# The scores of a compressed attention branch: keys in four column groups, queries moving, then two transposes

## The chip, the cores and the metric

The kernel runs on one core of one Trainium2 chip. The metric is the device time of one execution in microseconds (us); lower is better. Engines are named as in the profile: PE is TensorE, PEld its weight loads, DVE is VectorE, ACT is ScalarE, POOL is GpSimd, SP is SyncE, whose queue issues the weight DMAs.

## The reference, cut to what matters

The program is one block of a first architecture followed by two layers of a second one, on 256 tokens (S) of width 1024. Each layer of the second kind has a feed-forward part, a mixer with three attention branches, and a second feed-forward part. The change is in the mixer's second branch, in the part that attends to compressed keys:

```python
kc = rms_norm_2(nsa_compress(k_cmp, pe[0], w1[0], w2[0]), k_norm[0])   # (B, 15, 2 groups, 64)
kc = apply_rope(kc, cos_c, sin_c).transpose(0, 2, 1, 3)
...
sc = jnp.einsum('btghd,bgcd->bghtc', qb, kc) * scale     # 8 heads, 256 queries, 15 keys
pc = masked_softmax(sc, cmp_end[None, :] <= t_pos[:, None])
o_cmp = jnp.einsum('bghtc,bgcd->btghd', pc.astype(dt), vc)
```

So the scores are 8 heads by 256 queries by 15 compressed keys, with two key groups of four heads each, and the softmax runs over the 15 keys. They are computed once in each of the two layers, and all operands are float32.

## The kernel before, in words

**Weights.** All weights come in units of 1 MB that SP loads into three `raw` slots. ACT copies each into `w_hi` in a shortened format (`split_hi`, L253, 1.9 us), DVE subtracts that from the raw data into `w_lo` (`split_lo`, L260, 2.3 us), and PE multiplies with three products per tile (L818, L819, L820 in the projections). There are four slots of `w_hi` and `w_lo`. `ahead(i)` in the mixer is the split of unit u0+i+2; it stands at fixed places in the programs of ACT and DVE.

**Order.** Each engine has its own program, written out by hand, and runs it strictly in that order; the engines meet through semaphores. In `pe_mix2` the projections are cut into quarters of 12 matmuls (`quarter`, `tile`), and smaller work stands between them. `pe_items` transposes query and key pairs into PSUM banks 4 to 7, one bank for each item; ACT and DVE copy the items out in turn (`evac_items`, L886 on ACT, L888 on DVE, one with the even item numbers, the other with the odd ones). `pe_items_left` makes PE wait until all items are copied out. The next users of those banks are the attention scores.

**Around the change.** After quarter (6, 1, 0) PE waits for the copies of the first three query/key items, transposes two more (`qk_items[3:]`, six transposes at L868), computes the compressed scores (L1899), waits in `pe_items_left` and goes into `pe_attention`. There the step i issues the scores of block i (L908), `beside(i, 0)` (a quarter, then small work of the compressed branch), the transposes of the probabilities of block i-1 (L958), `beside(i, 1)` (another quarter), and the product with the values of block i-2 (L986).

The compressed scores before: for each of two token tiles and four head pairs one matmul with a 128x128 tile of queries (`qk_t[:, i, t*P:(t+1)*P]`) standing and `kc_t` moving. `kc_t` is 128 rows by 30 columns: rows 0 to 63 hold one group's 15 keys, rows 64 to 127 the other's, the rest is zero. The result lies in bank 3 as tokens by (head, key), as the softmax on DVE wants it (`cmp_shift`, L2269 to L2273, in DVE's step 0 after the maxima of block 0 (L919) and ahead of a weight split, L260).

On ACT the program runs here: copies of `qk_items[:3]` (L886), `ahead(12)` (L253), the copy of `qk_items[3:]` (L886), then in step 0 of the attention `ahead(13)` (L253) and the exponentials of block 0 (L928). On DVE: `evac_items` (L888), L1735, `ahead(12)` (L260), two gate operations, the maxima of block 0 (L919), `cmp_shift`, `ahead(13)` (L260), then step 1: reciprocals and scaled probabilities of block 0 (L998 to L1004). POOL zeroes `kc_t` at the start of the mixer (L1772), and ACT writes the transposed keys into it (L2035). The two layers differ in one thing that matters here: which of ACT and DVE has the even items, so the last item that ACT copies is 128x256 in the first layer and 128x512 in the second.

Other lines that the rows name: L1813 is the matmul in `hidden(k)`, four products with 32 standing columns each, placed in four column groups of the array by `tile_position`; L1922 is the pair of transposes of the compressed probabilities; L566 and L567 are the gate and up products of the first feed-forward part; L1188 and L1203 belong to the first block's attention; L423 is a residual addition.

Of the kernel before, what the change touches and what calls it, by code (L numbers as in the profile page):

```python
# [21 lines left out]
ALU = mybir.AluOpType  # L22
ACT = mybir.ActivationFunctionType
AX = mybir.AxisListType

P = 128
S = 256
NT = S // P
# [77 lines left out]
def build(nc, A, place, out):  # L106

    with ExitStack() as ctx:
# [18 lines left out]
        x = sb("x", [P, NT, D])  # L127
        tmp = sb("tmp", [P, 2176])
        qk_t = sb("qk_t", [P, 16, S])
# [9 lines left out]
        small = sb("small", [P, 656])  # L139
        forget_hi, forget_lo = (sb(f"forget_{i}", [P, KC * 8], F32R) for i in ("hi", "lo"))  # L140
        ps = ctx.enter_context(nc.psum_tensor("ps", [P, 8, 512], F32))
# [7 lines left out]
        def const(name, rows=P):  # L149
            a, w = place[name]  # L150
            return consts[0:rows, a:a + w]

        ident = const("ident")
# [46 lines left out]
        for ph in phases:  # L200
            ph = dict(ph)
# [675 lines left out]
        def evac_items(eng, st, items, parity, bank=0):  # L877
            for i, (srcs, dst, scale) in enumerate(items):
                m = st["item"] + i
                if m % 2 != parity:  # L880
                    continue
                eng.wait_ge(items_done, m + 1)
                n = len(srcs)
                src = ps[:, bank + i % 4, 0:n * S].rearrange("p (h s) -> p h s", h=n)
                if parity == 0:
                    nc.scalar.activation(dst, src, ACT.Copy, scale=scale).then_inc(item_act, 1)  # L886
                else:
                    nc.vector.tensor_scalar(dst, src, scale, None, ALU.mult).then_inc(item_dve, 1)  # L888
            st["item"] += len(items)
# [631 lines left out]
        SBH, NH, NG, DSH, IXH, IXD = 4, 8, 2, 4, 8, 32  # L1521
        NQ, NKC, NKS, NVS, NKW, NVW, GATES, DQ, DV0, IQ, IW = (768, 1280, 1536, 1664, 1792, 1920, 2048, 2072,
                                                               2392, 2456, 2744)
        NB = S // 16 - 1
# [14 lines left out]
        ptb = pt_buf[:, :, :, :].rearrange("p a b c -> p (a b c)")  # L1539
# [7 lines left out]
        kc_pair = small[0:2 * NB, 260:388]  # L1547
        kc_sq = small[0:2 * NB, 324:388]
        kc_ss = small[0:2 * NB, 388:389]
        kc_t = small[:, 390:390 + 2 * NB]  # L1550
        kc_rot = small[0:2 * NB, 420:452]
        nsa_gate = tiny(452, [NT, 3 * NH])
        gates = nsa_gate.rearrange("p t (h c) -> p t h c", c=3)
# [8 lines left out]
        cmp_s = qk_t[:, 11, 0:NT * NH * NB].rearrange("p (t h c) -> p t h c", t=NT, h=NH)  # L1562
# [4 lines left out]
        SIDE_BANK, CMP_BANK = 2, 3  # L1567

        def ev(name, ph):

            return sem(name), ph["mix2_before"] + 1

        def wait(eng, name, ph, times=1):
            s_, v_ = ev(name, ph)
            eng.wait_ge(s_, v_ * times)
# [193 lines left out]
            nc.gpsimd.memset(cmp_in[:, :, :, 2 * NB:32], 0.0).then_inc(ev("cmp_in_zeroed", ph)[0], 1)  # L1769

        def pool_mix2(pool, chain, ph):
            nc.gpsimd.memset(kc_t, 0.0).then_inc(ev("kct_zeroed", ph)[0], 1)  # L1772
            for i, (_, _, h0, n) in enumerate((qk_first, qk_second, qk_dsa)):
                ss = qk_ss[:, :, h0:h0 + n]
                pool.wait_ge(sem("qk_ss_ready"), 3 * ph["mix2_before"] + i + 1)
                nc.gpsimd.tensor_tensor(ss, ss, minus_half.unsqueeze(2).broadcast_to([P, NT, n]), ALU.pow)\
                    .then_inc(sem("qk_rstd_ready"), 1)
                if i == 0:
                    wait(pool, "kc_ss_ready", ph)
                    nc.gpsimd.tensor_tensor(kc_ss, kc_ss, minus_half[0:2 * NB], ALU.pow)\  # L1780
                        .then_inc(ev("kc_rstd_ready", ph)[0], 1)
            for t in range(NT):
                for h in range(2):
                    pool.wait_ge(sem("gated1"), 4 * ph["mix2_before"] + 2 * t + h + 1)
                    nc.gpsimd.tensor_tensor(xn[:, t, half(h)], gate_or_gain[:, t, half(h)],
                                            gate_or_gain[:, t, D + h * 512:D + (h + 1) * 512], ALU.add)\
                        .then_inc(sem("merged_ab"), 1)

        def pe_mix2(pe, ph):
# [44 lines left out]
            for a in range(2):  # L1834
                for g in range(NG):
                    for t in range(NT):
                        for par in range(2):
                            c = (a * NG + g) * P + t * HD
                            last = nc.tensor.matmul(ps[par * HD:(par + 1) * HD, SIDE_BANK, c:c + HD],
                                                    proj[:, t, NKC + (a * NG + g) * HD:NKC + (a * NG + g + 1) * HD],  # L1840
                                                    ident[:, par::2], start=True, stop=True)
# [20 lines left out]
                             start=True, stop=True)  # L1862
# [12 lines left out]
            for c in range(2):  # L1875
                for kt in range(NT):
                    for hh in range(2):
                        h = 2 * c + hh
                        last = nc.tensor.matmul(half_rows(o_sb[:, c, :], hh)[:, kt * P:S],
                                                proj[:, kt, 512 + h * HD:512 + (h + 1) * HD],  # L1880
                                                sb_view(pb, c)[:, hh, kt * S:kt * S + S - kt * P],
                                                start=kt == 0, stop=True, skip_group_check=True)
# [10 lines left out]
            wait(pe, "dk_ready", ph)  # L1893
            pe_items(pe, st, qk_items[3:], 4)
            wait(pe, "kcT_ready", ph, 2)
            for t in range(NT):
                for i in range(NH // 2):
                    c = (t * NH + 2 * i) * NB
                    last = nc.tensor.matmul(ps[:, CMP_BANK, c:c + 2 * NB], qk_t[:, i, t * P:(t + 1) * P],  # L1899
                                            kc_t, start=True, stop=True)  # L1900
            last.then_inc(ev("cmp_scores", ph)[0], 1)
            pe_items_left(pe, st)

            def branch(n, bank, first, last, t, rows_of=None):
# [5 lines left out]
            def beside(i, place):  # L1910
                j = 2 * i + place + 3
                if j < 24:
                    quarter(6 + j // 4, j % 4 // 2, j % 2)
                elif place == 0 and i > 10:
                    pe.wait_ge(proj_evac, pj0 + 24)
                    branch(23, 0, True, True, 0, "branch_rows0")
                if place:
                    return
                if i == 3:
                    wait(pe, "cmp_p_ready", ph)  # L1920
                    for t in range(NT):
                        last = nc.tensor.transpose(ps[0:NH * NB, CMP_BANK, t * P:(t + 1) * P],  # L1922
                                                   cmp_s[:, t].rearrange("p h c -> p (h c)"), ident)
                    last.then_inc(ev("cmp_pt", ph)[0], 1)
                if i in (4, 6, 8, 10):
                    c = i // 2 - 2
                    wait(pe, "cmp_pt_ready", ph)
                    nc.tensor.matmul(o_psum(c), v_diag.rearrange("p h d -> p (h d)")[:, c * P:(c + 1) * P], cmp_p_t,
                                     start=False, stop=True, skip_group_check=True).then_inc(sem("nsa_closed"), 1)
# [18 lines left out]
        def act_mix2(act, chain, ph):  # L1948
            st, u0, li = {"item": ph["item0"]}, ph["u0"], ph["mix2_before"]

            def ahead(i):
                split_hi(act, u0 + i + 2)
# [80 lines left out]
            for hh in range(2):  # L2033
                c = slice(hh * NB, (hh + 1) * NB)
# [5 lines left out]
            nc.scalar.activation(nsa_gate, nsa_gate, ACT.Exp, scale=-1.0).then_inc(ev("gates_exp", ph)[0], 1)  # L2040
            evac(6, 0)
            evac_items(act, st, qk_items[:3], 0, 4)
            ahead(12)
            evac_items(act, st, qk_items[3:], 0, 4)

# [36 lines left out]
        def dve_mix2(dve, chain, ph):  # L2082
# [81 lines left out]
            for a in range(2):  # L2164
                for g in range(NG):
                    c = (a * NG + g) * P
                    pairs = ps[:, SIDE_BANK, c:c + P].rearrange("p (m j) -> p m j", j=8)
                    for jh in range(2):
                        last = nc.vector.tensor_tensor(
                            cmp_in[:, a, 8 * jh:8 * jh + 8, g * NB:(g + 1) * NB].rearrange("p j c -> p c j"),  # L2170
                            pairs[:, jh:jh + NB, :],
                            cmp_pe[:, a, 8 * jh:8 * jh + 8].unsqueeze(1).broadcast_to([P, NB, 8]), ALU.add)
# [88 lines left out]

            shape = [P, NT, NH, NB]
            vis = const("cmpvis").rearrange("p (t c) -> p t c", t=NT).unsqueeze(2).broadcast_to(shape)
            bias = const("cmpbias").rearrange("p (t c) -> p t c", t=NT).unsqueeze(2).broadcast_to(shape)

            def cmp_shift():
                wait(dve, "cmp_scores", ph)
                sc = ps[:, CMP_BANK, 0:NT * NH * NB].rearrange("p (t h c) -> p t h c", t=NT, h=NH)
                chain(nc.vector.tensor_tensor(cmp_s, sc, bias, ALU.add))  # L2269
                chain.wait()  # L2270
                chain(nc.vector.tensor_reduce(cmp_max, cmp_s, AX.X, ALU.max))
                chain.wait()
                nc.vector.tensor_tensor(cmp_s, cmp_s, cmp_max.unsqueeze(3).broadcast_to(shape), ALU.subtract)\  # L2273
                    .then_inc(ev("cmp_shifted", ph)[0], 1)
# [17 lines left out]

            def beside(i, place):
                if place == 0:
                    if i == 0:
                        cmp_shift()
                    if i <= 10:
                        ahead(13 + i)
                    return
                if i == 1:  # L2300
                    cmp_softmax()
                if 1 <= i <= 5:
                    top_k(2 + i, 3 + i)
                if i == 6:
                    mask_from_taken()
# [204 lines left out]
```

## Time and profile before

| | |
|---|---|
| median of 3 runs | 1708.38 us (1708.22 to 1708.61) |
| the profiled execution | 1708.45 us, its span 1706.3 us |
| PE busy | 1694.1 us, 99% of the span |
| DVE busy | 1022.8 us, 60% |
| ACT busy | 840.0 us, 49% |
| POOL busy | 109.1 us, 6% |
| DMA | mean 176 GB/s |

The span is the time from the first to the last instruction that the profiler records; the run's own time has 2.15 us more around it. Busy shares are averages over the whole program; a matmul's duration in the trace runs to its modelled end, so matmuls that follow each other every 0.23 us have 0.39 us each.

### The profile page before, as it was taken

How to read it: one execution, taken by the hardware profiler on the slowest of the kernel's cores; microseconds unless marked ns; L12 is line 12 of the kernel's file. 1: busy time of each engine (PE TensorE's matmuls, PEld its weight loads, DVE VectorE, ACT ScalarE, POOL GpSimd, SP SyncE). 2: the span in 40 equal slices, each digit the busy share in tenths (PEclk: the TensorE clock that was granted, in tenths of full speed). 3: DMA queues.
4: the chain of work that ended last, by engine and by line, in shares of the span. 5: the costliest groups of instructions: out<-in, count | busy, mean ns of one | idle time of the engine just before them, and what ended most of it. 6: DMA issues, size and time to landing. Idle time of an engine off the chain costs nothing.

```text
span 1706.3 us, 22051 instructions
## 1 busy us (share of the span) xinstructions
PE 1694.1 (99%) x8308; PEld 1374.5 (81%) x8308; DVE 1022.8 (60%) x1481; ACT 840.0 (49%) x1102; POOL 109.1 (6%) x141
## 2 busy tenths in 40 slices
PE   8999999999999999999999999999999999999999
PEld 6888887788888888878778888888888787788887
DVE  6444756754556454769866545554547698665454
ACT  5444565643454343566664434443435666644342
POOL 2000200200003000100011000020001010110000
PEclk9999999999999999999999999999999999999999
DMA  8555542455557555534344554565555344345542
GB/s 296 184 202 176 173 173 99 166 193 196 180 190 232 195 185 184 197 107 159 131 136 170 189 197 175 195 229 198 176 192 195 104 156 138 129 171 194 197 172 99
DMA packets 69805, 299.87 MB, mean 176 GB/s; under 512 B 5408, under 2 KB 7680, under 8 KB 44512
## 3 DMA queue, kind: packets, MB, share of 16 engines
q1 hardware_dynamic: 66752, 291.52, 49.1%
q0 software_dynamic: 2688, 7.19, 1.4%
q8 instruction: 52, 0.85, 0.2%
q14 instruction: 25, 0.20, 0.0%
q10 hardware_dynamic: 288, 0.10, 0.0%
HBM read 297.74 MB, written 1.05 MB: 175 GB/s over the span
## 4 chain that ended last, share of the span: by engine, by line
PE 98%; DVE 1%; ACT 0%; DMA 0%; issue 0%; POOL 0%; ACTq 0%
PE ps L547 13%; PE ps L545 13%; PE ps L546 13%; PE ps L609 9%; PE ps L611 9%; PE ps L610 9%; PE ps L818 6%; PE ps L820 6%; PE ps L819 6%; PE ps L566 2%; PE ps L567 2%; PE ps L593 2%; PE ps L908 1%; PE ps L986 1%; PE ps L353 1%; PE ps L569 1%
## 5 line engine op out<-in xcount | busy, mean ns | idle before, releaser
L260 DVE TENSOR_TENSOR w_lo<-raw,w_hi 128x2048 fp32r<-128x2048 f32 x275 | 625.0, 2291 | 217.0 <-ACT w_hi L253 216.8
L253 ACT ACTIVATE w_hi<-raw 128x2048 fp32r<-128x2048 f32 x275 | 520.5, 1913 | 59.7 <-PE ps L820 32.5
L545 PE MATMUL ps<-w_hi,aT_hi 128*128 128x512 f32 x960 | 379.4, 395 | 0.0
L547 PE MATMUL ps<-w_hi,aT_lo 128*128 128x512 f32 x960 | 374.6, 390 | 0.0
L546 PE MATMUL ps<-w_lo,aT_hi 128*128 128x512 f32 x960 | 373.9, 389 | 0.0
L703 ACT ACTIVATE tmp<-ps,stats 128x256 f32<-128x256 f32 x132 | 62.6, 474 | 578.9 <-PE ps L547 568.6
L746 DVE TENSOR_TENSOR tmp<-tmp,ps 128x256 f32<-128x256 f32 x132 | 55.6, 421 | 337.4 <-ACT tmp L703 337.2
L609 PE MATMUL ps<-w_hi,act_hi 128*128 128x512 f32 x576 | 226.7, 394 | 0.1
L611 PE MATMUL ps<-w_hi,act_lo 128*128 128x512 f32 x576 | 224.4, 390 | 0.0
L610 PE MATMUL ps<-w_lo,act_hi 128*128 128x512 f32 x576 | 224.3, 389 | 0.0
L547 PEld LDWEIGHTS ps<-w_hi,aT_lo 128*128 128x128 f32 x960 | 180.2, 188 | 38.4
L546 PEld LDWEIGHTS ps<-w_lo,aT_hi 128*128 128x128 f32 x960 | 180.5, 188 | 36.0
L545 PEld LDWEIGHTS ps<-w_hi,aT_hi 128*128 128x128 f32 x960 | 180.4, 188 | 35.6
L818 PE MATMUL ps<-w_hi,aT_hi 128*128 128x512 f32 (+1 forms) x432 | 174.3, 404 | 0.0
L820 PE MATMUL ps<-w_hi,aT_lo 128*128 128x512 f32 (+1 forms) x432 | 165.4, 383 | 0.0
L819 PE MATMUL ps<-w_lo,aT_hi 128*128 128x512 f32 (+1 forms) x432 | 165.4, 383 | 0.0
L609 PEld LDWEIGHTS ps<-w_hi,act_hi 128*128 128x128 f32 x576 | 108.1, 188 | 23.2 <-issue 1.0
L611 PEld LDWEIGHTS ps<-w_hi,act_lo 128*128 128x128 f32 x576 | 108.1, 188 | 22.8
L610 PEld LDWEIGHTS ps<-w_lo,act_hi 128*128 128x128 f32 x576 | 108.2, 188 | 21.8
L818 PEld LDWEIGHTS ps<-w_hi,aT_hi 128*128 128x128 f32 x432 | 81.2, 188 | 27.0 <-issue 11.4
L820 PEld LDWEIGHTS ps<-w_hi,aT_lo 128*128 128x128 f32 x432 | 81.2, 188 | 16.8
L819 PEld LDWEIGHTS ps<-w_lo,aT_hi 128*128 128x128 f32 x432 | 81.4, 189 | 12.9
(296 smaller groups left out, 1605.5 us busy)
## 6 DMA issues: line engine op xcount, KB each, us to landing
raw<-in_ffn_units SPq DMA_DIRECT2D x197, 1024.0 KB, 5.0
raw<-in_w_in SPq DMA_DIRECT2D x34, 1024.0 KB, 5.2
raw<-in_w_gate SPq DMA_DIRECT2D x24, 1024.0 KB, 5.2
raw<-in_w_out SPq DMA_DIRECT2D x12, 1024.0 KB, 4.9
qk_t<-in_nsa_cmp_w POOLq DMA_DIRECT2D x8, 512.0 KB, 5.8
raw<-in_w_br_b SPq DMA_DIRECT2D x4, 1024.0 KB, 5.1
raw<-in_w_br_a SPq DMA_DIRECT2D x2, 1024.0 KB, 4.8
raw<-in_w_br_c SPq DMA_DIRECT2D x2, 1024.0 KB, 5.6
```

What stands on the lines that cost most here:

```text
L253: nc.scalar.activation(w_hi[w][:, :], raw[k][:, :], ACT.Copy).then_inc(hi_ready, 1)
L260: nc.vector.tensor_tensor(w_lo[w][:, :], raw[k][:, :], w_hi[w][:, :].bitcast(F32), ALU.subtract)\
L545: nc.tensor.matmul(dst, aT_hi[:, a, toks], hi[:, k, :], start=a == 0, stop=False)
L546: nc.tensor.matmul(dst, aT_hi[:, a, toks], lo[:, k, :], start=False, stop=False)
L547: last = nc.tensor.matmul(dst, aT_lo[:, a, toks], hi[:, k, :], start=False, stop=a == KC - 1)
L609: nc.tensor.matmul(dst, hi_a[:, c, toks], hi[:, c, cols], start=first and c == 0, stop=False)
L610: nc.tensor.matmul(dst, hi_a[:, c, toks], lo[:, c, cols], start=False, stop=False)
L611: mm = nc.tensor.matmul(dst, lo_a[:, c, toks], hi[:, c, cols], start=False, stop=last and c == 1)
L703: nc.scalar.activation(sg[par][:, t, :], gu(par, t)[:, 0, :], ACT.Silu, scale=rstd(ph, t))\
L818: nc.tensor.matmul(dst, aT_hi[:, a, toks], hi[:, k, :], start=a == 0, stop=False)
L819: nc.tensor.matmul(dst, aT_hi[:, a, toks], lo[:, k, :], start=False, stop=False)
L820: last = nc.tensor.matmul(dst, aT_lo[:, a, toks], hi[:, k, :], start=False, stop=a == KC - 1)
```

## The change

The compressed scores are computed the other way round. `kc_t` (now 32 columns wide, two of them zero) stands, in column group i of the array (`tile_position=(0, 32 * i)`), and all 256 queries of head pair i move; four such matmuls give bank 3 as (pair, key) by tokens. ACT copies this out (`cmp_flat`), and PE transposes it in two 128x128 transposes, after the first quarter in step 0 of the attention. `cmp_shift` on DVE reads these, in one addition for each token tile instead of one for both. `kc_t` moves to columns 80 to 111 of `small`, where `cmp_sig` was, and POOL zeroes it later, once the hidden values are done.

```diff
--- before.py
+++ after.py
@@ -1547,7 +1547,8 @@
         kc_pair = small[0:2 * NB, 260:388]
         kc_sq = small[0:2 * NB, 324:388]
         kc_ss = small[0:2 * NB, 388:389]
-        kc_t = small[:, 390:390 + 2 * NB]
+        kc_t = small[:, 80:112]
+        cmp_flat = ptb[:, 0:S]
         kc_rot = small[0:2 * NB, 420:452]
         nsa_gate = tiny(452, [NT, 3 * NH])
         gates = nsa_gate.rearrange("p t (h c) -> p t h c", c=3)
@@ -1769,13 +1770,14 @@
             nc.gpsimd.memset(cmp_in[:, :, :, 2 * NB:32], 0.0).then_inc(ev("cmp_in_zeroed", ph)[0], 1)
 
         def pool_mix2(pool, chain, ph):
-            nc.gpsimd.memset(kc_t, 0.0).then_inc(ev("kct_zeroed", ph)[0], 1)
             for i, (_, _, h0, n) in enumerate((qk_first, qk_second, qk_dsa)):
                 ss = qk_ss[:, :, h0:h0 + n]
                 pool.wait_ge(sem("qk_ss_ready"), 3 * ph["mix2_before"] + i + 1)
                 nc.gpsimd.tensor_tensor(ss, ss, minus_half.unsqueeze(2).broadcast_to([P, NT, n]), ALU.pow)\
                     .then_inc(sem("qk_rstd_ready"), 1)
                 if i == 0:
+                    wait(pool, "hid_ready", ph)
+                    nc.gpsimd.memset(kc_t, 0.0).then_inc(ev("kct_zeroed", ph)[0], 1)
                     wait(pool, "kc_ss_ready", ph)
                     nc.gpsimd.tensor_tensor(kc_ss, kc_ss, minus_half[0:2 * NB], ALU.pow)\
                         .then_inc(ev("kc_rstd_ready", ph)[0], 1)
@@ -1893,12 +1895,10 @@
             wait(pe, "dk_ready", ph)
             pe_items(pe, st, qk_items[3:], 4)
             wait(pe, "kcT_ready", ph, 2)
-            for t in range(NT):
-                for i in range(NH // 2):
-                    c = (t * NH + 2 * i) * NB
-                    last = nc.tensor.matmul(ps[:, CMP_BANK, c:c + 2 * NB], qk_t[:, i, t * P:(t + 1) * P],
-                                            kc_t, start=True, stop=True)
-            last.then_inc(ev("cmp_scores", ph)[0], 1)
+            for i in range(NH // 2):
+                last = nc.tensor.matmul(ps[32 * i:32 * i + 32, CMP_BANK, 0:S], kc_t, qk_t[:, i, :], start=True, stop=True,
+                                        tile_position=(0, 32 * i))
+            last.then_inc(ev("cmp_flat_done", ph)[0], 1)
             pe_items_left(pe, st)
 
             def branch(n, bank, first, last, t, rows_of=None):
@@ -1916,6 +1916,12 @@
                     branch(23, 0, True, True, 0, "branch_rows0")
                 if place:
                     return
+                if i == 0:
+                    wait(pe, "cmp_flat_ready", ph)
+                    for t in range(NT):
+                        last = nc.tensor.transpose(ps[:, CMP_BANK, S + t * P:S + (t + 1) * P],
+                                                   cmp_flat[:, t * P:(t + 1) * P], ident)
+                    last.then_inc(ev("cmp_scores", ph)[0], 1)
                 if i == 3:
                     wait(pe, "cmp_p_ready", ph)
                     for t in range(NT):
@@ -2040,6 +2046,8 @@
             nc.scalar.activation(nsa_gate, nsa_gate, ACT.Exp, scale=-1.0).then_inc(ev("gates_exp", ph)[0], 1)
             evac(6, 0)
             evac_items(act, st, qk_items[:3], 0, 4)
+            wait(act, "cmp_flat_done", ph)
+            nc.scalar.activation(cmp_flat, ps[:, CMP_BANK, 0:S], ACT.Copy).then_inc(ev("cmp_flat_ready", ph)[0], 1)
             ahead(12)
             evac_items(act, st, qk_items[3:], 0, 4)
 
@@ -2261,12 +2269,16 @@
 
             shape = [P, NT, NH, NB]
             vis = const("cmpvis").rearrange("p (t c) -> p t c", t=NT).unsqueeze(2).broadcast_to(shape)
-            bias = const("cmpbias").rearrange("p (t c) -> p t c", t=NT).unsqueeze(2).broadcast_to(shape)
+            bias = const("cmpbias").rearrange("p (t c) -> p t c", t=NT)
 
             def cmp_shift():
                 wait(dve, "cmp_scores", ph)
-                sc = ps[:, CMP_BANK, 0:NT * NH * NB].rearrange("p (t h c) -> p t h c", t=NT, h=NH)
-                chain(nc.vector.tensor_tensor(cmp_s, sc, bias, ALU.add))
+                sc = ps[:, CMP_BANK, S:2 * S].rearrange("p (t i x) -> p t i x", t=NT, i=NH // 2)
+                for t in range(NT):
+                    chain(nc.vector.tensor_tensor(cmp_s[:, t].rearrange("p (i g) c -> p i g c", g=2),
+                                                  sc[:, t, :, 0:2 * NB].rearrange("p i (g c) -> p i g c", g=2),
+                                                  bias[:, t].unsqueeze(1).unsqueeze(1).broadcast_to([P, NH // 2, 2, NB]),
+                                                  ALU.add))
                 chain.wait()
                 chain(nc.vector.tensor_reduce(cmp_max, cmp_s, AX.X, ALU.max))
                 chain.wait()
@@ -2292,11 +2304,11 @@
 
             def beside(i, place):
                 if place == 0:
-                    if i == 0:
-                        cmp_shift()
                     if i <= 10:
                         ahead(13 + i)
                     return
+                if i == 0:
+                    cmp_shift()
                 if i == 1:
                     cmp_softmax()
                 if 1 <= i <= 5:
```

## Rows read from the trace of the kernel before

**Rows 1.** The page: busy time of PE, its share of the span, instructions.

```profile
PE 1694.1 (99%) x8308; PEld 1374.5 (81%) x8308; DVE 1022.8 (60%) x1481; ACT 840.0 (49%) x1102; POOL 109.1 (6%) x141
```

**Rows 2.** Waits of PE: line waited for, us in total, times, longest us.

```profile
PE ps L353 <- DVE x L423: 1.3, 1, 1.3
```

**Rows 3.** Timeline of PE around the compressed scores: start us, us, what.

```profile
784.58 0.38 PE L868 MATMUL ps<-consts,qk_t 128*128 128x128 f32 x2
784.80 1.87 PE L1899 MATMUL ps<-small,qk_t 128*128 128x30 f32 x16
786.60 0.93 PE L908 MATMUL ps<-qk_t 64*128 64x128 f32 x8
...
790.29 0.39 PE L818 MATMUL ps<-w_hi,aT_hi 128*128 128x512 f32 x1
```

**Rows 4.** A wait of PE's sequencer: nanoseconds min/median/max, first and last start.

```profile
L935 PEldq EVENT_SEMAPHORE  x2: 867/892/918, 784.6 to 1382.6; - x2
```

**Rows 5.** Timeline of PE, a call of "hidden" between projection matmuls.

```profile
738.03 0.39 PE L819 MATMUL ps<-w_lo,aT_hi 128*128 128x512 f32 x1
738.26 0.40 PE L820 MATMUL ps<-w_hi,aT_lo 128*128 128x512 f32 x1
738.59 0.43 PE L1813 MATMUL ps<-qk_t,gate_or_gain 128*32 128x128 f32 x8
738.94 0.50 PE L818 MATMUL ps<-w_hi,aT_hi 128*128 128x512 f32 x1
```

**Rows 6.** PE groups by form: count, busy us, mean ns of one.

```profile
L986 PE MATMUL ps<-pt_buf,proj 128*64 128x128 f32 x96 | 9.3, 273 | 0.0
...
L1928 PE MATMUL ps<-qk_t 120*128 120x256 f32 x16 | 4.8, 378 | 0.0
```

**Rows 7.** Timeline of PE, two transposes ahead of six.

```profile
812.06 0.38 PE L1922 MATMUL ps<-consts,qk_t 128*120 128x128 f32 x2
812.28 0.82 PE L958 MATMUL ps<-consts,p_buf 128*128 128x128 f32 x6
```

**Rows 8.** Timeline of ACT in the first of the two layers.

```profile
785.00 0.38 ACT L886 ACTIVATE qk_t<-ps 128x256 f32<-128x256 f32 x1 [1.03 <-PE ps L868]
785.28 1.90 ACT L253 ACTIVATE w_hi<-raw 128x2048 fp32r<-128x2048 f32 x1
```

**Rows 9.** The producer and PE's first load after an ACT wait.

```profile
297.20 0.37 ACT L1203 ACTIVATE gate_or_gain<-ps 128x256 f32<-128x256 f32 x1
...
297.69 0.30 PEld L1188 LDWEIGHTS ps<-proj,pt_buf 128*128 128x128 f32 x2 [0.22 <-issue]
```

**Rows 10.** Timeline of DVE, first layer.

```profile
785.99 2.28 DVE L260 TENSOR_TENSOR w_lo<-raw,w_hi 128x2048 fp32r<-128x2048 f32 x1
...
790.01 0.40 DVE L2269 TENSOR_TENSOR qk_t<-ps,consts 128x240 f32<-128x240 f32 x1
...
791.21 2.29 DVE L260 TENSOR_TENSOR w_lo<-raw,w_hi 128x2048 fp32r<-128x2048 f32 x1
```

**Rows 11.** DVE, the second block of scaled probabilities.

```profile
802.49 1.01 DVE L1004 TENSOR_SCALAR p_buf<-p_buf,small 128x128 f32<-128x128 f32 x4
```

**Rows 12.** PE, the transposes that read them.

```profile
804.05 0.82 PE L958 MATMUL ps<-consts,p_buf 128*128 128x128 f32 x6
```

**Rows 13.** Timeline of PE and ACT in the second layer.

```profile
1382.60 0.38 PE L868 MATMUL ps<-consts,qk_t 128*128 128x128 f32 x2
...
1382.80 0.60 ACT L886 ACTIVATE qk_t<-ps 128x512 f32<-128x512 f32 x1 [1.24 <-PE ps L868]
...
1384.61 0.93 PE L908 MATMUL ps<-qk_t 64*128 64x128 f32 x8
```

**Rows 14.** The page's DMA issues: KB each, median us to landing.

```profile
raw<-in_w_gate SPq DMA_DIRECT2D x24, 1024.0 KB, 5.2
```

**Rows 15.** Timeline of PE at the start of the program.

```profile
10.94 0.63 PE L566 MATMUL ps<-w_hi,aT_hi 128*128 128x512 f32 x1
11.36 0.50 PE L567 MATMUL ps<-w_lo,aT_hi 128*128 128x512 f32 x1
```

## The prediction, made before the changed kernel ran

> **What bounds the kernel now.** I read the page's busy times first. PE is busy for 1694.1 us of a span of 1706.3 us [rows 1], so the time is PE's time, and a change is worth what it adds to or takes from PE's row of work. Next I read who makes PE wait: after the start of the program the longest wait is 1.3 us [rows 2], so nearly nothing can be won by waiting less, and a new wait shows in full. Then the timeline of PE around the edit. The compressed scores are 16 records, two for each of 8 float32 matmuls. From the second of the two L868 transposes (784.69, one pitch of 0.11 after 784.58) to the first score of the attention (786.60) there are 1.91 us [rows 3]. Last I looked at what else ends there: PE's sequencer sits at the waits of `pe_items_left` and L935 for 0.92 us from 784.60, so until 785.52 [rows 4]. That wait costs nothing today, because the 16 queued records keep the array busy until 786.60. It is the row that decides this case.
>
> **What the new matmuls cost PE.** No row has four 32-column groups with 256 moving columns; the nearest has them with 128. There 8 records start and end within 0.36 us, 738.59 to 738.94 [rows 5], so the four groups run beside each other. Entering the mode costs 0.10 (738.26 to 738.59 is 0.33 against a pitch of 0.23 for 738.03 to 738.26). From 128 to 256 columns a record grows by 0.10 to 0.11 (273 ns to 378 ns [rows 6]), in two rounds, so the block takes 0.36 + 0.21 = 0.57, and its last result lies ready 0.43 + 0.21 = 0.64 after its start. Lower bound of the block: 0.36, as if the columns were free. Upper bound: eight records one after another at 0.21 each, 1.70. I take 0.57, as the row is the same form but for its length.
> The Trainium skill ("TensorEngine Tiling (Array Packing)", Key Properties) says that changing the tiling mode drains the engine; rows 5 show it, 0.10 on the way in, and that is in the sum.
> Start of the block: 784.69 + 0.11 + 0.10 = 784.90. PE would be through at 785.47, 1.13 us earlier than before. That is what the edit takes away.
>
> **What it adds on PE.** Two transposes in step 0 of the attention. A pair takes 0.22 (812.06 to 812.28 [rows 7]) in the same mode as its neighbours, so 0.22 per layer. Were this all, each layer would gain 0.91 us.
>
> **The wait that comes up.** PE must not begin the scores before `pe_items_left`, so not before ACT has copied its last item out of PSUM. ACT runs its program in order, and the edit puts two things ahead of that copy: a wait for the new matmuls, and the copy of their result. But `ahead(12)`, the 1.90 us split, already stood between the first copies and the last one. Before, ACT did that split while PE worked on a quarter, and then idled for 1.03 us until the last item came [rows 8]. Now ACT stands before the split, waiting for PE. Queued behind the waiting copy are the split, the last item's copy, and PE behind that. First layer:
> - matmul result 784.90 + 0.64 = 785.54; ACT starts 0.04 later, as it did after L868 (784.58 + 0.38 to 785.00 [rows 3, 8]), at 785.58;
> - the copy of 128x256 from PSUM: the next instruction starts 0.28 after such a one (785.00 to 785.28 [rows 8]), 785.86;
> - the split: 1.90 [rows 8], less the 0.10 by which neighbours overlap (0.38 against 0.28), 787.66;
> - the last item's copy, 128x256: 0.38 [rows 8], 788.04;
> - to PE's first load after a copy by ACT that it waited for: 297.20 + 0.37 to 297.69, 0.12 [rows 9], 788.15.
> The scores started at 786.60 before [rows 3], so PE is now 1.55 us later, after standing still for 788.15 - 785.47 = 2.7 us.
> Second layer, same steps from 1382.60 + 0.11 + 0.20 = 1382.91: result and ACT's start +0.68, copy +0.28, split +1.80, gives 1385.67. ACT's last item is 128x512 here and takes 0.60 [rows 13]: 1386.27, PE at 1386.38 or so. Before it was 1384.61 [rows 13]: 1.77 us later.
> Bounds of this term: with the block at 0.36 both layers are 0.21 less; with it serial, 1.13 more. The copy cannot overtake the split, so I know of no lower end but that of the rival below.
> The Trainium skill's tiling page (Performance Considerations, PSUM Bottleneck) warns that after a fourfold gain on TensorE the copy out of PSUM may become the bound. By that rule alone the copy's 0.28 to 0.38 would be the price and the layer would still gain; the trace says that the copy is the small part and the 1.80 queued behind it the large one.
>
> **What is hidden.** The last-item delay also moves DVE. Its `ahead(12)` (L260) starts at 785.99 [rows 10] and needs ACT's split, now done at 785.86 + 1.90 = 787.76; it starts at 787.80, 1.81 later. The score maxima follow and end 1.81 later, so `cmp_shift` could start at 790.01 + 1.81 = 791.82 [rows 10]. The two transposes end later: the second quarter of step 0, ahead of which they stand, began at 790.29 [rows 3], now 791.84, they add 0.22 and their latency, 792.2. So DVE waits another 0.4, and its addition, split in two of half the size, costs 0.1 more. `ahead(13)`, at 791.21 before [rows 10], comes some 2.3 later, and all behind it too, DVE having no gap there. PE is later itself by 1.55 + 0.22 = 1.77, so DVE loses 0.5 us against PE. The tightest meeting is in step 2: the scaled probabilities of block 1 run from 802.49 to 803.50 [rows 11], their first half done at about 803.0, and PE takes them at 804.05 [rows 12]. A margin of 1.0 shrinks to 0.5, which holds; without that cover it would cost up to 0.5 a layer per further 1.0 of DVE delay. The weight units have more room: the unit split by `ahead(12)` is used from the second quarter after the second scores on, some 9 us after its split. SP's next load starts when DVE frees the raw slot, 1.8 later, and lands in 5.2 [rows 14], about 795.3, some 5 us ahead of ACT's need in step 2. POOL's zeroing of `kc_t` moves behind the first of its powers; POOL is busy for 6% of the span [rows 1], the write into `kc_t` comes two projection tiles later, and nobody waits for the zeroing. Nothing is priced there.
>
> **The sum.** First layer 1.55 + 0.22, second 1.77 + 0.22: 3.76 us more. The profiled execution has 1706.3 + 2.15 = 1708.45, which is within 0.1 of the median of the runs, 1708.38. Forecast: 1708.38 + 3.76 = 1712.1.
>
> **The rivals.**
> *A. The wait is hidden; not slower.* PE gains 1.13 - 0.22 = 0.91 a layer and the time is 1706.6. It needs ACT's last copy to be done by the time PE leaves the new block: the chain of copy, split and copy would have to be 2.7 us shorter, so the decisive point is whether 788.15 falls below 785.47. For it: before, the same wait was hidden (rows 4). Against it: hidden by the very records that go, and ACT's order is written out. 9 in 100.
> *B. The column groups don't run together at 256 columns.* Then the block takes 1.70, 1.13 more; ACT starts later by that, and with it PE: 3.76 + 2.26, 1714.4. For it: four groups read four different query tiles of 256 columns at once, which no row shows. Against it: rows 5. 5 in 100.
> *C. TensorE's clock falls in the wait.* At the start of the program matmuls of 512 columns follow each other at 0.42 (10.94 to 11.36 [rows 15]), the 1.2 GHz level, against 0.23 later (rows 5), the 2.4 GHz level. If each wait brought the low level back for 4 us, a length I assume, half of that would be lost twice: 1716. For it: waits of 2.7 and 2.9 us are twice the longest that rows 2 hold, and by the Trainium skill ("TensorE: Matmul & The Clock Gate", HAM oscillation) idle gaps that are long enough bring the low clock back. Against it: over the 1.3 us the granted clock stayed at 1.0, and the array is full on both sides. 3 in 100.
> *D. DVE makes PE wait once more.* If its delay is 1 us over what I have, the margin of 0.5 is gone and each layer loses another 0.5: 1713.1. 5 in 100.
>
> **How the numbers follow.** The forecast's own case has 78 in 100; its range is 3.3 to 4.3 above before, 1711.7 to 1712.7, from 0.2 less on the block or the hand-over to some 0.3 of DVE's lag. A measurement tells 0.2% from no change, 3.4 us here, and the forecast is only 0.3 above that. So of the 78 I give 58 to slower and 20 to within. With B, C and D slower is 71; with A (0.11% faster, so within) within is 28; 1 is left for faster. The range from 1710.8 to 1714.8 holds the forecast's case, D and B; A and C are left out.
>
> **What would show each step.** In the trace after: eight records with 32 standing columns within about 0.6 us (else B); PE idle for 2.7 us in the first layer and 2.9 in the second ahead of L908, with an ACT copy (L886) as the releaser; on ACT the new copy, then L253 at once, then L886; DVE's `ahead(12)` starting right at the end of that L253; matmuls at a pitch of 0.23 behind the wait (else C); no new wait of PE at the transposes of step 2 (else D). The prediction is wrong if PE's idle time before L908 is under 2 us in either layer, or if any wait over 0.3 us appears elsewhere.

## The result, and the profile after

The changed kernel takes 1716.8 us in the median of 6 runs (1714.67 to 1717.31), against 1708.3 us (1707.98 to 1708.61) for the kernel before on the same chip: a ratio of 1.0046, 95% interval 1.0036 to 1.0056. It is slower, as forecast, but by 8.5 us and not by 3.8, outside the range of 1710.8 to 1714.8. The profiled execution is the slowest of the six, 1717.31 us with a span of 1715.2 us.

The page of the changed kernel, to be read against [rows 1]. PE is busy for 3.5 us more, although it runs 12 matmul records fewer:

```profile
PE 1697.6 (99%) x8296; PEld 1375.2 (80%) x8296; DVE 1024.1 (60%) x1483; ACT 840.9 (49%) x1104; POOL 109.0 (6%) x141
```

Its waits of PE (line waited for, us in total, times, longest us). One line is new, and the others are those of before ([rows 2] among them):

```profile
PE ps L908 <- ACT qk_t L886: 5.4, 2, 2.8
...
PE ps L353 <- DVE x L423: 1.3, 1, 1.3
```

The timeline of PE in the first layer (start us, us, engine, line, what). This answers to [rows 3]; everything here is 0.70 later, from the start of the program, so compare distances:

```profile
785.28 0.38 PE L868 MATMUL ps<-consts,qk_t 128*128 128x128 f32 x2
785.59 0.64 PE L1899 MATMUL ps<-qk_t,small 128*32 128x256 f32 x8
788.80 1.46 PE L908 MATMUL ps<-qk_t 64*128 64x128 f32 x8 [2.58 <-ACT qk_t L886]
790.19 0.79 PE L818 MATMUL ps<-w_hi,aT_hi 128*128 128x512 f32 x1
790.78 0.63 PE L819 MATMUL ps<-w_lo,aT_hi 128*128 128x512 f32 x1
791.21 0.63 PE L820 MATMUL ps<-w_hi,aT_lo 128*128 128x512 f32 x1
...
792.48 0.39 PE L820 MATMUL ps<-w_hi,aT_lo 128*128 128x512 f32 x1
792.71 0.39 PE L818 MATMUL ps<-w_hi,aT_hi 128*128 128x512 f32 x1
...
794.08 0.38 PE L1922 MATMUL ps<-consts,pt_buf 128*128 128x128 f32 x2
```

From the second L868 transpose (785.39) to the first score (788.80) there are 3.42 us, where there were 1.91. In the middle PE stands idle. Then comes what I had not put in the forecast: after the wait the 512-column matmuls follow each other at 0.43 us (790.78 to 791.21) and only from 792.48 on at 0.23.

ACT in the same stretch, against [rows 8]: it waits 3.43 us for PE, copies the scores out (L2050), does the weight split (L253), and only then copies the last item (L886), for which PE waits.

```profile
786.29 0.38 ACT L2050 ACTIVATE pt_buf<-ps 128x256 f32<-128x256 f32 x1 [3.43 <-PE ps L1899]
786.57 1.90 ACT L253 ACTIVATE w_hi<-raw 128x2048 fp32r<-128x2048 f32 x1
788.37 0.38 ACT L886 ACTIVATE qk_t<-ps 128x256 f32<-128x256 f32 x1
```

DVE in the same stretch, against [rows 10]. It idles for 1.74 us until ACT's split is done; counted from the second L868 transpose its own split starts 3.12 us later, where it was 1.30, so 1.82 us late (forecast 1.81). `cmp_shift` (L2278) stands behind the next split, no longer ahead of it:

```profile
788.51 2.29 DVE L260 TENSOR_TENSOR w_lo<-raw,w_hi 128x2048 fp32r<-128x2048 f32 x1 [1.74 <-ACT w_hi L253]
...
792.54 2.29 DVE L260 TENSOR_TENSOR w_lo<-raw,w_hi 128x2048 fp32r<-128x2048 f32 x1
794.74 0.47 DVE L2278 TENSOR_TENSOR qk_t<-ps,consts 128x120 f32<-128x120 f32 x2
```

Stretches of the changed kernel (from:to in us, length, then busy time of PE, PEld, DVE, ACT and POOL with counts, the granted clock, DMA share, GB/s): the wait, what follows it, and what follows that, for the first and then the second layer:

```profile
786.24:788.81 2.57, 0.01 (x2) 0.01 (x2) 0.83 (x2) 2.52 (x4) 0.00 (x0) 1.00 0.92 324
789.10:792.40 3.30, 3.30 (x13) 2.25 (x11) 3.23 (x10) 2.03 (x4) 0.00 (x0) 0.50 0.22 32
792.50:796.00 3.50, 3.50 (x18) 2.86 (x17) 3.43 (x7) 1.87 (x7) 0.00 (x0) 1.00 0.78 286
1387.61:1390.39 2.78, 0.00 (x0) 0.00 (x0) 0.99 (x2) 2.72 (x4) 0.00 (x0) 0.89 0.81 251
1390.40:1396.60 6.20, 6.20 (x19) 4.58 (x20) 5.73 (x12) 3.62 (x9) 0.00 (x0) 0.50 0.67 224
1396.70:1400.00 3.30, 3.30 (x16) 2.43 (x15) 2.47 (x10) 1.91 (x3) 0.00 (x0) 1.00 0.78 236
```

The third number from the end is the granted clock. 0.50 is the 1.2 GHz level, for at least 3.3 us in the first layer and 6.2 us in the second, while PE is busy all the time; ahead of it PE had idled for 2.6 and 2.8 us. In the second layer the clock fell while PE still waited (0.89 is a mean over the wait); in the first it fell only once PE was busy again (1.00 over the whole wait). Behind each low stretch it is at 1.00, 2.4 GHz.

A ledger helps. I cut each trace at the same instructions: a is the last transpose ahead of the compressed scores, b the first attention score, c the first matmul of the feed-forward part behind the mixer.

| from, to | before | changed | difference |
|---|---|---|---|
| start to a, layer 1 | 784.69 | 785.39 | +0.70 |
| a to b, layer 1 | 1.91 | 3.42 | +1.51 |
| b to c, layer 1 | 132.52 | 134.39 | +1.87 |
| c to a, layer 2 | 463.59 | 463.57 | -0.02 |
| a to b, layer 2 | 1.91 | 3.63 | +1.72 |
| b to c, layer 2 | 132.56 | 135.71 | +3.15 |
| c to the last matmul | 185.54 | 185.54 | 0.00 |

The sum is 8.9 us, the difference of the spans (1715.2 - 1706.3). The 0.70 at the start belongs to this one execution: e3 and e6 below have the same code up to a, and reach it after 784.60 and 784.67. All else of the loss lies within the two mixers.

### The profile page after: what moved, and what is told of

The parts are those of the page before. It is cut to its first block, busy times and chain, and to the rows that moved or that the text cites. A ratio compares the mean times of both kernels' runs of the same rounds, so it can differ in the third digit from the quotient of the medians.

```text
span 1715.2 us, 22031 instructions
## 1 busy us (share of the span) xinstructions
PE 1697.6 (99%) x8296; PEld 1375.2 (80%) x8296; DVE 1024.1 (60%) x1483; ACT 840.9 (49%) x1104; POOL 109.0 (6%) x141
## 4 chain that ended last, share of the span: by engine, by line
PE 98%; DVE 1%; ACT 1%; DMA 0%; issue 0%; POOL 0%; ACTq 0%
PE ps L547 13%; PE ps L545 13%; PE ps L546 13%; PE ps L609 9%; PE ps L611 9%; PE ps L610 9%; PE ps L818 6%; PE ps L819 6%; PE ps L820 6%; PE ps L566 2%; PE ps L567 2%; PE ps L593 2%; PE ps L908 1%; PE ps L986 1%; PE ps L353 1%; PE ps L569 1%
## 5 line engine op out<-in xcount | busy, mean ns | idle before, releaser
L260 DVE TENSOR_TENSOR w_lo<-raw,w_hi 128x2048 fp32r<-128x2048 f32 x275 | 625.2, 2292 | 220.3 <-ACT w_hi L253 220.1
L253 ACT ACTIVATE w_hi<-raw 128x2048 fp32r<-128x2048 f32 x275 | 520.5, 1913 | 59.9 <-PE ps L820 32.5
```

Of the source, the lines that this page charges most:

```text
L253: nc.scalar.activation(w_hi[w][:, :], raw[k][:, :], ACT.Copy).then_inc(hi_ready, 1)
L260: nc.vector.tensor_tensor(w_lo[w][:, :], raw[k][:, :], w_hi[w][:, :].bitcast(F32), ALU.subtract)\
```

## The experiments

Every kernel computes the same function except `e6_one_group`. Ratios are to the kernel before, run on the same chip.

### e3_fill: the same wait, but with PE at work

```diff
             last.then_inc(ev("cmp_flat_done", ph)[0], 1)
+            pe.wait_ge(proj_evac, pj0 + 13)
+            for _ in range(5):
+                for i in range(NH // 2):
+                    nc.tensor.matmul(ps[32 * i:32 * i + 32, 0, 0:S], kc_t, qk_t[:, i, :], start=True, stop=True,
+                                     tile_position=(0, 32 * i))
             pe_items_left(pe, st)
```

> The changed kernel, with five more sets of the same four matmuls (into bank 0, which is free there; their result isn't used) behind the new block, so that PE works while it waits for ACT. The wait ends when it did. Theory (an idle PE is what brings the low clock): the clock stays at 1.000, only the later start is left, 1.55 and 1.77 us and twice 0.22: 1712.1. Rival (the clock falls for another reason, such as the light load of matmuls with 32 standing columns, or the lost 4.7 us are somewhere else): 1716.8 as in the changed kernel.

The added `wait_ge` holds PE until bank 0 is copied out. Measured: 1712.22 us (1711.67 to 1712.59, 10 runs), ratio 1.0022 (1.0012 to 1.0031). PE's timeline shows 40 records of useless work (line 1905 of its code) behind the block, then a rest of 0.42 us of idle time, then the scores.

```profile
784.49 0.38 PE L868 MATMUL ps<-consts,qk_t 128*128 128x128 f32 x2
784.80 0.64 PE L1899 MATMUL ps<-qk_t,small 128*32 128x256 f32 x8
785.26 2.34 PE L1905 MATMUL ps<-qk_t,small 128*32 128x256 f32 x40
788.01 0.93 PE L908 MATMUL ps<-qk_t 64*128 64x128 f32 x8 [0.42 <-ACT qk_t L886]
788.87 0.50 PE L818 MATMUL ps<-w_hi,aT_hi 128*128 128x512 f32 x1
789.21 0.40 PE L819 MATMUL ps<-w_lo,aT_hi 128*128 128x512 f32 x1
789.44 0.39 PE L820 MATMUL ps<-w_hi,aT_lo 128*128 128x512 f32 x1
```

From a (784.60) to b (788.01) there are 3.42 us, as in the changed kernel, so the wait is the same; but 789.21 to 789.44 is the fast pitch. From b to c it takes 132.78 in both layers. PE does more work than in the changed kernel and the program is 4.6 us faster. That settles it: the wait itself costs what was forecast (1712.1), and the rest of the loss comes from the clock, which falls when PE idles through the wait and stays up when it works. It also splits the b-to-c rows of the ledger: e3's are 0.26 and 0.22 us longer than before, which is the transposes, so 1.61 and 2.93 us are left for the clock.

### e4_before_stall, e5_shorter_wait, e9_wait_13: the old matmuls, with a wait of chosen length

The kernel before, with ACT copying its last item again and again, each copy waiting for the one before (nine and six times more in e4, seven and five in e5, six and four in e9; the two numbers are for the item of the first and of the second layer):

```diff
                 if parity == 0:
+                    for _ in range(again[n] if again else 0):
+                        again["chain"](nc.scalar.activation(dst, src, ACT.Copy, scale=scale))
+                        again["chain"].wait()
                     nc.scalar.activation(dst, src, ACT.Copy, scale=scale).then_inc(item_act, 1)
...
-            evac_items(act, st, qk_items[3:], 0, 4)
+            evac_items(act, st, qk_items[3:], 0, 4, {1: 9, 2: 6, "chain": chain})
```

> The kernel before, in which ACT copies its last query/key item ten times (seven in the second layer), so that PE, with the old matmuls, stands idle for some 2.7 us ahead of the attention scores; all results as before. Theory (the length of the idle time alone brings the low clock): 5.4 us for the two waits, and 1.7 to 3.4 a layer for the clock, 1717 to 1720. Rival (the low clock comes from the new form of the matmuls): 1713.7 with a clock of 1.000.

> The kernel before with fewer repeated copies of ACT's last item (eight and six in all), so that PE idles for about 1.8 us in each layer where e4 had 2.5. Theory (a wait must be long enough before the clock falls; 1.2 us waits left it alone, 2.5 us ones didn't): somewhere between, the extra goes to the waits' own 3.7 us. If 1.8 us is short enough, 1712.1 and a clock of 1.000; if not, one stretch or two at the low level, 1.5 to 3 us each, 1714 to 1718. Rival (any wait at this place lowers the clock in proportion): about 0.7 of e4's 4 us, 1715.

> The kernel before with seven and five copies of ACT's last item, for an idle time of PE of about 1.3 us in each layer. So far waits of 1.2 us left the clock alone and waits of 1.8 us brought the low level in both layers. Theory (the wait must be long enough): 2 x 1.3 us, 1711.0 and a clock of 1.000 if 1.3 us is short enough, one or two stretches and 1.5 us each on top, 1712.5 to 1714.1, if not. Rival (in e5 it was not the idle time but the repeated copies on ACT): the low level here as well, with 1.5 us in each layer.

Measured: e4 1718.09 us (ratio 1.0057, 1.0042 to 1.0073), e5 1715.88 us (1.0047, 1.0031 to 1.0062), e9 1714.39 us (1.0036, 1.0022 to 1.0050). By stretches, in the profiled executions:

| | PE idle before b, layers 1 and 2 | b to c over before, layer 1 | layer 2 |
|---|---|---|---|
| e4 | 2.50, 2.53 | +2.61 | +1.45 |
| e5 | 1.67, 1.91 | +1.57 | +1.56 |
| e9 | 1.26, 1.28 | +0.05 | +1.44 |

The scores of e9 in the first layer, then in the second, from its timeline of PE (in its code this is line 911):

```profile
787.63 0.93 PE L911 MATMUL ps<-qk_t 64*128 64x128 f32 x8 [1.26 <-ACT qk_t L889]
```

```profile
1387.04 1.65 PE L911 MATMUL ps<-qk_t 64*128 64x128 f32 x8 [1.28 <-ACT qk_t L889]
```

Eight records take 0.93 us in one layer and 1.65 us in the other, behind waits of nearly the same length. The low stretches of e4, first and second layer:

```profile
789.50:795.10 5.60, 5.60 (x18) 4.08 (x19) 3.74 (x12) 3.61 (x9) 0.00 (x0) 0.50 0.59 187
1392.70:1395.90 3.20, 3.18 (x12) 2.24 (x13) 1.39 (x9) 2.76 (x6) 0.00 (x0) 0.50 0.90 303
```

And e5, the wait and what follows, with the clock third from the end:

```profile
786.50:788.30 1.80, 0.17 (x2) 0.06 (x1) 1.80 (x2) 1.67 (x6) 0.00 (x0) 1.00 1.01 395
788.30:789.10 0.80, 0.76 (x8) 0.52 (x8) 0.52 (x2) 0.80 (x1) 0.00 (x0) 1.00 0.39 149
789.20:792.50 3.30, 3.30 (x10) 2.62 (x9) 3.02 (x12) 2.64 (x9) 0.00 (x0) 0.50 0.85 290
792.70:796.00 3.30, 3.30 (x16) 2.75 (x15) 2.57 (x7) 2.20 (x3) 0.00 (x0) 1.00 0.29 46
```

The new form of matmul isn't needed for it: the old ones get the same low clock. Nor are the repeated copies on ACT: the changed kernel has none, and in e9's first layer they stand ahead of a wait that left the clock alone.

The loss isn't in proportion to the wait either. A wait of 1.67 us cost 1.57 us of clock, one of 2.58 us in the changed kernel cost 1.61; the clock falls to the low level or not at all, and what sets the loss is how long it stays there. In e4 two waits of 2.50 and 2.53 us cost 2.61 and 1.45 us, as the low stretch lasts at least 5.6 us behind one and 3.2 us behind the other. Why one stretch is longer than another is open.

For e5's time alone both expectations would do, 1715.9 against 1714 to 1718 and 1715; the comparison of wait and loss tells them apart. In e9 my theory's clean version, short waits are free, fails: the five runs lie between 1712.21 and 1715.11, so none is at the 1711.0 of an undisturbed clock, and in the profiled one the clock fell in one layer and not in the other. At 1.3 us the length alone doesn't say whether it falls. The wait of 1.3 us in [rows 2] says so too: it stands in all eleven traces of this case, 1.27 us each time, and never brought the low level. In the kernel before:

```profile
317.30:318.55 1.25, 0.00 (x1) 0.01 (x1) 0.90 (x3) 0.69 (x2) 0.40 (x1) 1.00 0.75 177
```

What decides, if not the length, is open.

### e1_copy_last: no wait

```diff
-            wait(act, "cmp_flat_done", ph)
-            nc.scalar.activation(cmp_flat, ps[:, CMP_BANK, 0:S], ACT.Copy).then_inc(ev("cmp_flat_ready", ph)[0], 1)
             ahead(12)
             evac_items(act, st, qk_items[3:], 0, 4)
+            wait(act, "cmp_flat_done", ph)
+            nc.scalar.activation(cmp_flat, ps[:, CMP_BANK, 0:S], ACT.Copy).then_inc(ev("cmp_flat_ready", ph)[0], 1)
```

> The changed kernel, with ACT's copy of the new scores moved behind the weight split and behind the copy of the last query/key item; PE, DVE and POOL as changed. Theory (all of the loss is PE waiting for ACT's last item, and the clock that falls in that wait): both waits go, each layer keeps 1.13 us from the shorter block less 0.22 for the transposes, so 1.8 us under the kernel before, 1706.5, and the granted clock is 1.000. Rival (the new matmuls or the transposes themselves cost time, or lower the clock): at or over the kernel before, 1708.3 or more, with stretches at the low level.

Measured: 1707.04 us (1706.41 to 1707.87, 11 runs), ratio 0.9991 (0.9982 to 1.0000), 1.4 us under the kernel before. PE and then ACT, each from its timeline:

```profile
785.63 0.38 PE L868 MATMUL ps<-consts,qk_t 128*128 128x128 f32 x2
785.94 0.64 PE L1899 MATMUL ps<-qk_t,small 128*32 128x256 f32 x8
786.62 0.93 PE L908 MATMUL ps<-qk_t 64*128 64x128 f32 x8
```

```profile
783.11 1.91 ACT L253 ACTIVATE w_hi<-raw 128x2048 fp32r<-128x2048 f32 x1
786.05 0.38 ACT L886 ACTIVATE qk_t<-ps 128x256 f32<-128x256 f32 x1 [1.03 <-PE ps L868]
786.65 0.38 ACT L2052 ACTIVATE pt_buf<-ps 128x256 f32<-128x256 f32 x1 [0.21 <-PE ps L1899]
786.93 1.91 ACT L253 ACTIVATE w_hi<-raw 128x2048 fp32r<-128x2048 f32 x1
```

The split runs at 783.11 while PE works on a quarter; the last item is out at 786.43; a to b is 0.88 us (0.84 in the second layer) where it was 1.91. Moving the copy behind the split and the last item on ACT turns the loss into a gain.

The gain is 1.4 us and not the 1.8 that I expected. Of the 0.4, 0.16 lies in a to b, for which the forecast was 1.91 - 1.13 = 0.78: the first weight load for the scores still waits for the last item's copy, which the queued matmuls no longer cover.

```profile
786.59 0.55 PEld L908 LDWEIGHTS ps<-qk_t 64*128 64x128 f32 x8 [0.50 <-ACT qk_t L886]
```

The other 0.24 lies in b to c, which is 0.36 and 0.32 us longer than before where 0.22 was counted (e7 looks into it).

### e6_one_group: what the column groups are worth

e1 with the four matmuls in one column group; three quarters of the scores are left out.

```diff
-                last = nc.tensor.matmul(ps[32 * i:32 * i + 32, CMP_BANK, 0:S], kc_t, qk_t[:, i, :], start=True, stop=True,
-                                        tile_position=(0, 32 * i))
+                last = nc.tensor.matmul(ps[0:32, CMP_BANK, 0:S], kc_t, qk_t[:, i, :], start=True, stop=True,
+                                        tile_position=(0, 0))
```

> e1_copy_last with all four matmuls of the compressed scores in column group 0, one behind the other and over each other's result, so that three quarters of the scores are left out. It prices what the column groups save. Theory (the groups run beside each other, so alone they save 1.13 us a layer): 1707.0 + 2.3 = 1709.3, and from the last of the transposes ahead of the block to the first attention score 2.0 us instead of 0.88. Rival (the block is short because only 8 records stand where 16 were, the groups add nothing): 1707.0.

Measured: 1708.97 us, ratio 1.0004 (0.9994 to 1.0013). Its block, to be held against the 0.64 us above:

```profile
784.56 0.38 PE L868 MATMUL ps<-consts,qk_t 128*128 128x128 f32 x2
784.87 1.91 PE L1899 MATMUL ps<-qk_t,small 128*32 128x256 f32 x8
786.72 0.93 PE L908 MATMUL ps<-qk_t 64*128 64x128 f32 x8
```

The same eight records take 1.91 us, as long as the old sixteen (1.87 [rows 3]); a to b is 2.05 against 0.88. So the groups run beside each other and they are the whole gain; turning the matmul round by itself would only have added the transposes. Rival B is out. (The four also write over each other here; that this isn't what holds them apart wasn't run by itself.)

### e2_split_last and e8_split_last_topk_later: a short wait, and DVE

e2 puts ACT's last item behind the new copy, with the weight split behind both; e8 is e2 with the top-k rounds of DVE one step later.

```diff
             wait(act, "cmp_flat_done", ph)
             nc.scalar.activation(cmp_flat, ps[:, CMP_BANK, 0:S], ACT.Copy).then_inc(ev("cmp_flat_ready", ph)[0], 1)
-            ahead(12)
             evac_items(act, st, qk_items[3:], 0, 4)
+            ahead(12)
```

```diff
-                if 1 <= i <= 5:
-                    top_k(2 + i, 3 + i)
+                if 2 <= i <= 6:
+                    top_k(1 + i, 2 + i)
```

> The changed kernel, with the copy of the last query/key item put directly behind ACT's copy of the new scores, and the weight split behind both. PE still waits for ACT, but without the 1.80 us split: about 0.9 us of idle PE in the first layer and 1.1 in the second. Theory: PE starts the attention scores within 0.3 us of the time before, and the transposes add 0.22 a layer, so 1708.5, and idle times this short leave the clock at 1.000. Rival (any idle time behind the new block brings the low clock): 1.7 us or more on top in each layer, 1712 or more.

> e2_split_last with each round of the top-k search on DVE one step later. In e2 PE waited 1.15 us in each layer for the scaled probabilities (L1004) of block 1, as DVE was late by the weight split and had no gap. Theory (DVE's lag is the price in e2): 1.4 us of DVE work less ahead of L1004, so that both waits go and 2.3 us come back, 1709.2. Rival (L1004 is late because ACT's exponentials are late): the wait stays, 1711.5.

Measured: e2 1711.47 us, ratio 1.0017 (1.0008 to 1.0026): 3 us over what I expected, with a clock of 1.000, so by neither theory. Its waits of PE give the reason:

```profile
PE ps L958 <- DVE p_buf L1004: 2.3, 2, 1.2
...
PE ps L908 <- ACT qk_t L886: 1.8, 2, 1.0
```

Behind the wait that I had counted (L908) stands one that I hadn't: in each layer PE waits 1.15 us for the scaled probabilities of block 1. ACT's split is even later here than in the changed kernel, by 0.27 us counted from a, DVE's split with it, DVE has no gap until then, and PE is no longer late itself. This is rival D of the prediction, in a kernel where PE's own delay doesn't cover it. e8 shows that it is DVE: 1708.71 us (ratio 1.0001, 0.9992 to 1.0010), the wait is gone, and b to c falls from 134.28 to 132.87 and 132.82. Its expectation was 1709.2. Also, waits of 0.8 to 1.15 us, four to a run, left the clock at 1.000 in every run of e2.

### e7_topk_later: e1 with DVE relieved

The same top-k edit on e1.

> e1_copy_last with each round of the top-k search on DVE one step later (steps 2 to 6 instead of 1 to 5). Theory (in e1 the stretch behind the first attention score is 0.34 us a layer longer than before, 0.22 for the transposes and 0.1 for DVE's lag in steps 1 and 2): up to 0.1 us a layer is won, 1706.8. Rival (the 0.1 is in the chain of matmuls around the transposes): no difference, 1707.0; if the search, now all behind step 2, comes late for the mask, slower.

Measured: 1706.80 us (1706.40 to 1707.70, 11 runs), ratio 0.9992 (0.9983 to 1.0001). b to c is 132.84 and 132.80, where e1 has 132.88 twice: 0.1 us in all, too little for the times to tell. e1 and e7 are the versions to keep. They beat both kernels, the one before by 1.4 to 1.7 us or 0.1%, with intervals that just reach no change. The ledger's stretches, which aren't blurred by the program's start, show that both mixers are shorter: in e1 by 1.03 - 0.36 and 1.07 - 0.32 us.

## Why the prediction was wrong

- **The block.** Forecast 0.64 us to its last result, from 0.21 after the last transpose's start. Measured 0.64, and 0.20 (785.39 to 785.59). Right.
- **The wait.** Forecast 3.46 and 3.67 us from a to b. Measured 3.42 and 3.63, released by ACT's L886 in both layers. Right, with its cause: the split queued between the two copies. By e3 the forecast without the clock holds to 0.1 us of the time, 1712.22 against 1712.1.
- **The transposes.** Forecast 0.22 a layer. Measured 0.26 and 0.22, as what e3's b to c gained. Right.
- **The clock: the step that failed.** The sum took the clock as staying at its high level through waits of 2.7 and 2.9 us, and gave rival C 3 in 100. It fell in both layers and cost 1.61 and 2.93 us in the profiled run. Of the signs that the prediction named, this one appeared: matmuls at 0.43 behind the wait and not at 0.23. The case against C was one row, a wait of 1.3 us with the clock at 1.0 [rows 2]. It shows one such wait that passed; e9 shows that waits of the same length need not pass, and both waits of the forecast were twice as long. Rival C's own price, 2 us a layer and 1716, was nearly the result, in part by luck: its assumed 4 us of low clock lie between the two stretches that came, of at least 3.3 and 6.2 us. The Trainium skill ("TensorE: Matmul & The Clock Gate", HAM oscillation) warns that idle gaps which are long enough bring the low clock back. The runs here agree with that, and show it for gaps shorter than the forecast's own: in e5 the clock fell behind waits of 1.67 and 1.91 us. The limit that the page sets for such gaps is longer than any wait here; the measurement decides.
- **DVE's order: misread, without effect on the sum.** I placed `cmp_shift` ahead of `ahead(13)`. The edit moves it behind (L2278 at 794.74, behind L260 at 792.54). So DVE didn't wait for the transposes; the same work still stood ahead of the scaled probabilities, and no wait of PE arose (D didn't happen in the changed kernel, nor in e3, where no low clock delays PE; e2 has it).
- **Rival A** was the right kind of kernel in the wrong place: by e1 it is the order of a few lines in ACT's program away.

The chances came out on the right side (slower), the range did not: it left out a rival that had only a single, shorter wait against it.

## What to carry to other kernels

When an edit shortens the work of an engine that is always busy, first list what that work covers: here a sequencer's wait of 0.92 us that cost nothing, and behind it another engine's 1.90 us instruction. On an in-order engine, a new hand-over belongs behind everything that the waiting engine still needs, not where its data is first ready. And price each new idle microsecond of TensorE twice, once for itself and once for the clock: here waits of 2.6 and 2.8 us cost 1.6 and 2.9 us more, and useless matmuls in the waits were 4.6 us faster than none.

## What the runs showed of the hardware

- Waits of TensorE and the granted clock that followed: 0.8 to 1.15 us, stayed at 1.00 (e2, all 11 runs); 1.27 us at another place, stayed in all eleven traces ([rows 2]); 1.26 and 1.28 us, stayed once and fell once in one run (e9, whose five runs all have a mean clock under 1.000); 1.67 us and more, fell in each of the six that were profiled (e4, e5, the changed kernel). The low stretches cost 1.4 to 2.9 us each.
- The same kernel can pay for a short low stretch or a long one: one run of the changed kernel took 1714.67 us with a mean clock of 0.998, the other five 1716.46 to 1717.31 with 0.997.
- Four float32 matmuls with 128 rows, 32 standing columns and 256 moving ones take 0.64 us in four column groups (the changed kernel) and 1.91 us in one (e6).
